# A fused hybrid layer on one core: projection in segments of two, two and four blocks, the first one in the query weights' room

## The chip, the core and the metric

The kernel runs on one core of a Trainium2 chip as one launch. The metric is the device time of that core in microseconds. Before the change the median of three runs is 3722.16 us (3713.23 to 3744.35).

## The reference: what is computed

One layer over 1024 tokens of width 1024, float32, cut here to its stages:

```python
h = rms_norm(x, norm1_w)
proj = h @ w_in                     # 1024 -> 3592 columns
sq, sk = rms_norm(q), rms_norm(k)   # 8 attention heads of 64
o_sb  = rms_norm(stick_breaking_attention(sq, sk, sv))
qkv   = silu(causal_depthwise_conv(gdn_qkv))          # 4 taps
gq, gk = l2_normalize(gq) * 128**-0.5, l2_normalize(gk)
o_gdn = rms_norm(gated_delta_net(gq, gk, gv, decay, write)) * silu(gate)
x = x + concat(o_sb, o_gdn) @ w_out
hn = rms_norm(x)
q = hn @ peer_w_q                   # 8 heads x 2 halves x 128
# top 16 of 128 keys per half, top 16 of the 256 sums -> 128 experts per token
act = gelu(u_table[experts] . hn) * softmax(best)
y = x + sum(act * v_table[experts])
```

Attention is causal over blocks of 128 tokens, the delta net carries a state from block to block, and the convolution needs the last three tokens of the columns before. Every token reads 128 rows of 4 KB from the table u and 128 from v.

## The kernel before, in words

**Tiles.** The 1024 tokens are 8 blocks of 128. Two blocks form a segment (`SEG = 2`, line 38), so there are four segments. `projection(g)` computes all input projections of a segment and writes them to scratch tensors in device memory (`d_gqT`, `d_gkT`, `d_gv`, `d_qT`, `d_kT`, `d_v`, `d_gate`, `d_ab`). `mixing(b)` then runs one block: delta net ("start", "level", "state" in the list of points), attention over b+1 key blocks ("key"), output projection ("mix", "out"), the second norm ("hn"), the query projection with the resident 8 MB of `w_q` and the key scores ("pq", "score"), and the top-16 selections ("top"). The order is segment 0, blocks 0 and 1, segment 1, blocks 2 and 3, segment 2, and so on.

**A projection step.** The 3584 columns are 28 chunks of 128 (`CH`, line 46), of the kinds g (query and key of the delta net), v, s (attention query and key), a (attention value) and z (gate). One step is one chunk for the two blocks: 8 matmuls with a result of 128 x 256, an evacuation on ACT, for g and v a convolution of four taps on DVE, for g, v and z a silu on ACT and DVE, for g and s a norm. These stages trail the matmul by one to six steps, and nine more steps drain them. Weights come in pairs of chunks of 1 MB. Segment 0 reads them from `w_in` in runs of 1 KB through four slots and also saves them to `d_w`; later segments read them back from `d_w` through two slots. SP issues all of these loads and stores in one order: the load of pair j+2 is issued when pair j is through the matmuls, behind the stores of the steps before.

**Room.** `work` (24 tiles of 512 columns) holds a segment's tiles during a projection and a block's tiles during mixing, so the loads of block 0's delta net wait for the whole projection (line 537). `w_q_t` is filled after segment 0 and scaled once by the second norm's weights on ACT (line 951).

**Gathers.** POOL issues 1024 gathers from u and 1024 from v, one column of indices each: 128 rows of 4 KB, 512 KB. DVE takes each u row block's dot product with the normed tokens (line 1072) and frees its slot of `u_ring` (9 slots). PE sums the v rows with weights that ACT spreads into `column`, and frees its slot of `v_ring` (8 slots). The gathers of block b are spread by a table over the work on later blocks: `points()` gives every place in the program a weight, `MARKS` (line 144) gives pairs of (block, share of its stretch, u rows done, v rows done), and `table()` interpolates. At each point DVE, ACT, PE and POOL process rows up to the table's number. After block 7 only rows are left ("last"). Every engine runs its instructions strictly in this written order.

**Ahead of a segment.** In the "top" part of the block before, the segment's token blocks are loaded, squared, scaled and turned (`x_loads`, `x_squares`, `x_scale`, `x_turns`, `x_copies`); PE waits in `x_turns` for the scaled blocks.

Of the kernel before, what the change touches and what calls it, by code (L numbers as in the profile page):

```python
# [36 lines left out]

SEG = 2
ST = SEG * P
NSEG = NB // SEG  # L40
# [3 lines left out]
NP = len(PAIRS)  # L44

# [7 lines left out]
def number(kinds, n):  # L53
    return sum(CH[m][0] in kinds for m in range(n + 1))


def conv_count(n):
    return number("gv", n)


def silu_count(n):
    return number("gvz", n)


def norm_count(n):
    return number("gs", n)


Z0 = min(n for n in range(NCH) if CH[n][0] == "z")


def needs_tokens(n):
    return CH[n][0] == "v"


def stored(n):
    return CH[n][0] != "v"


def token_count(n):  # L80
    return sum(needs_tokens(m) for m in range(n + 1))


def stores_before(n, slot):
    return sum(stored(m) for m in range(slot, n, 4))


NORMS, CONVS, SILUS, TOKS = norm_count(NCH - 1), conv_count(NCH - 1), silu_count(NCH - 1), token_count(NCH - 1)
# [30 lines left out]
def segment_before(b):  # L119

    return b // SEG if b >= 2 and b % SEG == 0 else None


def token_turn_pending(n):

    return any(0 <= m < NCH and needs_tokens(m) for m in (n - 7, n - 8))


def points():


    for b in range(1, NB):
        if segment_before(b) is not None:
            for n in range(NCH + 9):
                yield ("p", segment_before(b), n), 5.0 if n < NCH else 2.5, None if n < 4 or token_turn_pending(n) else 1
# [8 lines left out]
MARKS = [(1, 0.62, 128, 0), (1, 1.0, 128, 40), (2, 1.0, 250, 118), (4, 1.0, 500, 368), (6, 1.0, 756, 624), (7, 1.0, 884, 750)]  # L144
# [57 lines left out]
def hybrid_layer_kernel(nc, x, norm1_w, w_in, sb_q_norm_w, sb_k_norm_w, sb_out_norm_w, gdn_conv_w,  # L202
# [9 lines left out]
    d_w = scratch("d_w", (NP, P, KC * 256))  # L212
# [12 lines left out]
    with ctx:  # L225
# [53 lines left out]

        xT = work[:, 0:KC * ST].rearrange("p (k t) -> p k t", k=KC)  # L280
        w_work = [work[:, 2048 * n:2048 * (n + 1)].rearrange("p (k c) -> p k c", k=KC) for n in (2, 1)]
        v_flat = v_ring[:, :, :].rearrange("p s d -> p (s d)")
        w_v = [v_flat[:, 2048 * n:2048 * (n + 1)].rearrange("p (k c) -> p k c", k=KC) for n in range(PW_FIRST - PW)]
        w_slots = [w_work[0], *w_v, w_work[1]]
        A0 = 6144

        def tile_a(n):
            return work[:, A0 + n * ST:A0 + (n + 1) * ST]


        x_seg = work[:, 2048:2048 + SEG * D].rearrange("p (n d) -> p n d", n=SEG)
        x_scratch = work[:, 0:D]
        s_ring = [tile_a(n) for n in range(6)] + [tile_a(20)]
        e_ring = [tile_a(6 + n) for n in range(2)]
        sq_ring = [tile_a(8 + n) for n in range(2)]
        y_ring = [tile_a(10 + n) for n in range(2)]
        o_ring = [tile_a(12 + n) for n in range(4)]
        tok_ring = [tile_a(16 + n) for n in range(2)]
        tmp_a = [tile_a(18), tile_a(19)]
        cb = [work[:, A0 + 21 * ST + n * 264:A0 + 21 * ST + n * 264 + ST + 3] for n in range(2)]  # L300
# [4 lines left out]
        ab_bank = bank(ox, 1)[:, 0:16]  # L305
        AB = A0 + 21 * ST + 2 * 264
        ab_out, ab_e = work[:, AB:AB + 16], work[:, AB + 16:AB + 32]
        ab_y = work[:, AB + 32:AB + 40]
        ab3 = ab_bank.rearrange("p (b c) -> p b c", b=SEG)
        ab_y3, ab_e3 = ab_y.rearrange("p (b c) -> p b c", b=SEG), ab_e[:, 8:16].rearrange("p (b c) -> p b c", b=SEG)  # L310
        ab_o3 = ab_out.rearrange("p (b c) -> p b c", b=SEG)

        u_flat = u_ring[:, :, :].rearrange("p s d -> p (s d)")
# [158 lines left out]
        def w_slot(g, j):  # L472
            return w_slots[slot_of(g, j)[0]]
# [1334 lines left out]
```

## Time and profile before

| | |
|---|---|
| median of three runs | 3722.16 us |
| the profiled execution | 3719.36 us, of which the span is 3717.5 us |
| granted TensorE clock, mean | 0.774 |
| busy, of the span | PE 66%, DVE 63%, POOL 62%, ACT 23% |
| bytes moved | 1267.87 MB, 341 GB/s over the span |
| the gathers' queue | 1073.87 MB, 77.1% of 16 DMA engines' time |

The DMA share is the mean busy share of the core's 16 DMA engines; it can pass 1 where several queues' packets overlap. A stage's row gives busy microseconds and, in brackets, the number of instructions of each engine in that stretch. POOL's number counts the gathers it issued. The stretches start and end at marks in the trace: segments at the block before's last selection, blocks at the first operation of their delta net.

### The profile page before, as it was taken

What the parts mean: (1) busy time and instruction counts of PE and PEld (TensorE: products, weight loads), DVE (VectorE), ACT (ScalarE), POOL (GpSimd) and SP (SyncE); (2) the same over time, 40 slices, a digit from 0 to 9 for tenths busy, and PEclk for the clock granted to TensorE, in tenths of its full rate; (3) what the DMA queues carried; (4) which work ended last, traced back from release to release, by engine and by line L of the source; (5) the groups of instructions that cost most, each with busy time, mean ns of one, the idle gap of its engine ahead of it and who ended that gap; (6) DMA issues with size and microseconds to landing.
All of it is one profiled execution on the core that took longest, in us unless ns stands there. A gap on an engine that the chain in (4) does not pass through costs nothing.

```text
span 3717.5 us, 46890 instructions
## 1 busy us (share of the span) xinstructions
PE 2447.1 (66%) x16321; PEld 1511.2 (41%) x16321; DVE 2333.5 (63%) x5581; ACT 862.8 (23%) x2400; POOL 2323.0 (62%) x2091
## 2 busy tenths in 40 slices
PE   7672546967747858668657868568757863544466
PEld 6562433644524536344434546344434440100123
DVE  4439875777676577666777677656876567444300
ACT  4330112332113123223114223223113211110112
POOL 0004774565556667766666766766777777777765
PEclk9786577988867979788778979788767785555588
DMA  7725998998889999999989999999999999999999
GB/s 242 252 77 191 338 327 312 348 361 310 306 281 367 357 345 413 406 387 384 359 319 392 345 369 414 404 365 363 348 331 391 370 330 356 377 364 376 355 375 336
DMA packets 392250, 1267.87 MB, mean 341 GB/s; under 512 B 43789, under 2 KB 95058, under 8 KB 382802
## 3 DMA queue, kind: packets, MB, share of 16 engines
q0 software_dynamic: 294912, 1073.87, 77.1%
q1 hardware_dynamic: 78674, 149.06, 11.1%
q10 hardware_dynamic: 18432, 41.95, 3.1%
q8 instruction: 132, 2.16, 0.2%
q14 instruction: 100, 0.82, 0.1%
HBM read 1225.89 MB, written 38.83 MB: 340 GB/s over the span
## 4 chain that ended last, share of the span: by engine, by line
PE 33%; DVE 24%; issue 12%; POOL 12%; DMA 6%; another core or an unknown queue 6%; ACT 3%; DVEq 3%; ACTq 1%; SPq 0%; POOLq 0%
PE zz L1520 16%; PE va L1520 10%; DVE u_ring L1072 8%; POOL u_ring L683 7%; POOL v_ring L698 5%; PE rr L1520 4%; DMA v_ring<-in_peer_v,idxT 3%; PE ox L1520 2%; DMA u_ring<-in_peer_u,idx 2%; DMA work<-d_w 1%; DVE work L1405 1%; DVE work L1407 1%; DVE work L1129 1%; DVE work L1288 1%
## 5 line engine op out<-in xcount | busy, mean ns | idle before, releaser
L683 POOL DMA_INDIRECT u_ring<-in_peer_u,idx x1024 | 1187.1, 1159 | 856.0 <-issue 293.0
L1072 DVE SCALAR_TENSOR_TENSOR u_ring<-u_ring,hn_t 128x1024 f32<-128x1024 f32 x1024 | 1216.9, 1222 | 316.4 <-DMA u_ring<-in_peer_u,idx 270.0
L698 POOL DMA_INDIRECT v_ring<-in_peer_v,idxT x960 | 1066.8, 1111 | 497.2 <-issue 234.1
L1520 PE MATMUL va<-v_ring,column 128*32 128x256 f32 x7680 | 809.3, 479 | 518.2 <-DMA v_ring<-in_peer_v,idxT 329.8
L1520 PE MATMUL zz<-work 128*128 128x256 f32 (+3 forms) x3232 | 738.5, 390 | 128.4 <-issue 50.5
L1520 PEld LDWEIGHTS zz<-work 128*128 128x128 f32 (+1 forms) x3232 | 551.9, 212 | 339.6 <-issue 202.7
L1520 PEld LDWEIGHTS va<-v_ring,column 128*32 128x32 f32 x7680 | 247.8, 124 | 1009.7 <-DMA v_ring<-in_peer_v,idxT 484.6
L762 ACT ACTIVATE column<-onehot,wT 128x32 f32<-128x32 f32 x1024 | 279.4, 314 | 917.0 <-PE va L1520 513.3
L1520 PE MATMUL rr<-work,w_q_t 128*128 128x128 f32 x1024 | 140.7, 291 | 18.5 <-issue 17.4
L1520 PE MATMUL rr<-work,later 128*128 128x512 f32 x144 | 102.3, 818 | 76.6 <-issue 35.2
L1520 PEld LDWEIGHTS rr<-work,w_q_t 128*128 128x128 f32 x1024 | 130.8, 204 | 31.2 <-issue 29.9
L1520 PE MATMUL zz<-work,w_q_t 128*128 128x128 f32 x1024 | 127.9, 283 | 8.0 <-issue 7.7
L1476 DVE TENSOR_TENSOR y_buf<-va,y_buf 128x1024 f32<-128x1024 f32 x8 | 9.8, 1221 | 194.4 <-PE va L1520 194.0
L1520 PEld LDWEIGHTS zz<-work,w_q_t 128*128 128x128 f32 x1024 | 122.1, 198 | 18.5 <-issue 18.5
L1520 PE MATMUL rr<-work 128*128 128x128 f32 x640 | 102.5, 314 | 22.2 <-DVE work L1244 6.7
L1520 PE MATMUL ox<-work 128*128 128x64 f32 (+1 forms) x704 | 99.8, 298 | 20.1 <-ACT work L931 18.9
L1520 PEld LDWEIGHTS ox<-work 128*128 128x128 f32 x704 | 92.8, 211 | 42.2 <-issue 42.0
L1520 PEld LDWEIGHTS rr<-work 128*128 128x128 f32 x640 | 93.2, 225 | 36.2 <-issue 15.7
L1524 PE MATMUL zz<-ident,work 128*128 128x128 f32 x40 | 11.3, 428 | 146.2 <-DVE work L1414 83.6
L1270 DVE SCALAR_TENSOR_TENSOR work<-zz,work 128x512 f32<-128x512 f32 x72 | 49.4, 686 | 77.8 <-ACT work L923 43.9
L1277 DVE SCALAR_TENSOR_TENSOR work<-zz,work 128x512 f32<-128x512 f32 x72 | 49.3, 685 | 55.4 <-remote 37.4
L1072 DVE DVE_READ_ACCUMULATOR u_ring<-u_ring,hn_t 128x1 f32 x1024 | 83.1, 81 | 0.0
(247 smaller groups left out, 2513.2 us busy)
## 6 DMA issues: line engine op xcount, KB each, us to landing
work<-d_w SPq DMA_DIRECT2D x42, 1024.0 KB
work<-in_w_out ACTq DMA_DIRECT2D x64, 512.0 KB
u_ring<-in_peer_u,idx POOLq DMA_INDIRECT x1024
v_ring<-in_peer_v,idxT POOLq DMA_INDIRECT x960
work<-d_kT SPq DMA_DIRECT2D x36, 256.0 KB
work<-d_v SPq DMA_DIRECT2D x36, 256.0 KB
work<-in_x SPq DMA_DIRECT2D x16, 512.0 KB
w_q_t<-in_peer_w_q SPq DMA_DIRECT2D x1, 8192.0 KB, 27.3
```

The costliest lines, as they stand in the source:

```text
L683: g.indirect_dma_start(u_ring[:, n % RU, :], None, u_rows, bass.IndirectOffsetOnAxis(idx[b % 2][:, s:s + 1], 0)).then_inc(u_landed[n % RU] ...
L698: g.indirect_dma_start(v_row(n), None, v_rows, bass.IndirectOffsetOnAxis(idxT[b % 3][:, t:t + 1], 0)).then_inc(v_landed[slot] if slot < RV ...
L762: a.activation(column[:, m % RC, :], onehot[:, 31 - g:63 - g], ACT.Copy, scale=wT[b % 2][:, 32 * k + g:32 * k + g + 1]).then_inc(column_do ...
L1072: v.scalar_tensor_tensor(u_ring[:, m % RU, :], u_ring[:, m % RU, :], 1.0, hn_t[b % 2][:, :], ALU.mult, ALU.mult, accum_out=dots[:, s:s + 1 ...
L1129: last = v.scalar_tensor_tensor(s_ring[n % 7], cb[c % 2][:, k:k + ST], vecs[:, w[k]:w[k] + 1], s_ring[n % 7], ALU.mult, ALU.add)
L1270: sp = v.scalar_tensor_tensor(att_sp[hg], bank(zz, hg), 0.0, att_l[hg], ALU.max, ALU.add)
L1277: v.scalar_tensor_tensor(att_u[hg], bank(zz, hg), 0.0, att_l[hg], ALU.min, ALU.subtract).then_inc(z_used, 1)
L1288: arg = v.tensor_tensor(att_u[hg], att_u[hg], bank(rr, hg), ALU.subtract)
L1405: v.tensor_tensor(hot[half], hot[half], top_f[:, of, c, :].unsqueeze(2).to_broadcast(shape), ALU.mult)
L1407: v.tensor_reduce(e[:, of], hot[half], AX.X, ALU.add)
L1520: return t_.matmul(out_, lhsT, rhs, start=start, stop=stop, skip_group_check=True)
L1524: last = t_.transpose(dst[:, c * P:(c + 1) * P], src[:, c * P:(c + 1) * P], ident[:, :])
```

## The change

The segments are 2, 2 and 4 blocks (`SIZES`). A step stays one chunk of 128 columns for two blocks; the segment of four runs every chunk twice, once for each pair of blocks ("halves"), so it has 56 steps plus 9. Its weights come from `d_w` as single chunks of 512 KB, each used by two steps. `d_w` is now stored by chunk. For the kinds a and z a step was 256 columns of one block; now it is 128 columns of both, in 16 matmuls of 128 columns instead of 8 of 256. The tiles of a segment are an `Area`: segment 0's lies in `w_q_t`, the others' in `work`. Block 0's delta-net loads are issued once the g and v chunks are stored; `w_q` is loaded after the projection, and is no longer scaled: instead the turned hidden state is scaled when it is copied, in four operations on ACT and four on DVE in every block. The turns of the two sub-key tables move from after segment 0 into block 0's mixing. The four token blocks of the last segment are prepared in block 3's selections. `MARKS` has new entries.

```diff
-SEG = 2
-ST = SEG * P
-NSEG = NB // SEG
+SIZES = (2, 2, 4)
+B0 = [sum(SIZES[:g]) for g in range(len(SIZES) + 1)]
+NSEG = len(SIZES)
+ST = 2 * P
...
-MARKS = [(1, 0.62, 128, 0), (1, 1.0, 128, 40), (2, 1.0, 250, 118), (4, 1.0, 500, 368), (6, 1.0, 756, 624), (7, 1.0, 884, 750)]
+MARKS = [(1, 0.62, 128, 0), (1, 1.0, 128, 40), (2, 1.0, 250, 118), (3, 1.0, 339, 207), (4, 1.0, 500, 374), (6, 1.0, 744, 596),
+         (7, 1.0, 884, 750)]
...
-    d_w = scratch("d_w", (NP, P, KC * 256))
+    d_w = scratch("d_w", (NCH, P, KC * P))
...
+                if size == 2:
+                    self.xT = [columns(base[:, 0:2048], ST)]
+                    self.w_slots = [base[:, 4096:6144], v_flat[:, 0:2048], v_flat[:, 2048:4096], base[:, 2048:4096]]
+                else:
+                    self.xT = [columns(base[:, 0:2048], ST), columns(base[:, 4096:6144], ST)]
+                    self.w_slots = [base[:, 2048:3072], None, None, base[:, 3072:4096]]
...
+        areas = [Area(w_q_t if g == 0 else work, SIZES[g]) for g in range(NSEG)]
...
                 if j >= ahead:
-                    sp.wait_ge(projected, NCH * g + 2 * (j - ahead) + 2)
-                elif j == ahead - 1:
-                    sp.wait_ge(x_turned, SEG * (g + 1))
+                    sp.wait_ge(projected, G.steps0 + 2 * (j - ahead) + 2)
+                elif j == ahead - 1 or G.halves == 2:
+                    sp.wait_ge(x_turned, B0[g + 1])
...
+                    for c in range(2):
+                        sp.dma_start(columns(w_slot(g, j)[:, 1024 * c:1024 * c + 1024], P),
+                                     w_in[0].rearrange("(k p) n -> p k n", p=P)[:, :, col + P * c:col + P * c + P]).then_inc(
+                                         w_landed[slot], 8 * 2)
+                elif G.unit == 2:
+                    sp.dma_start(columns(w_slot(g, j), KC * P),
+                                 d_w[2 * j:2 * j + 2].rearrange("h p c -> p h c")).then_inc(w_landed[slot], 16)
                 else:
-                    src = d_w[j].rearrange("p (k c) -> p k c", k=KC)
-                sp.dma_start(w_slot(g, j), src).then_inc(w_landed[slot], 16)
+                    sp.dma_start(w_slot(g, j), d_w[j]).then_inc(w_landed[slot], 16)
...
-                    if n == Z0 + 4:
-                        sp.wait_ge(projected, NCH * (g + 1))
...
+                    if g == 0 and n == G.gv_end + 5:
...
+                        gdn_loads(0)
+                    if g and n == G.steps:
...
             def x_scale(g):
                 act.wait_ge(x_meaned, 2 * g + 2)
-                for n in range(SEG):
-                    a.activation(x_seg[:, n, :], x_seg[:, n, :], ACT.Copy, scale=r8[:, n:n + 1]).then_inc(x_scaled, 1)
+                for n in areas[g].x_order:
+                    x = areas[g].x_rows[n]
+                    a.activation(x, x, ACT.Copy, scale=r8[:, n:n + 1]).then_inc(x_scaled, 1)
...
-                if b == 0:
-                    act.wait_ge(wq_landed, 16)
-                    for k in range(KC):
-                        a.activation(w_q_sb[:, k, :], w_q_sb[:, k, :], ACT.Copy, scale=vecs[:, R_N2 + k:R_N2 + k + 1])
...
-                a.activation(hT[:, 0:512], bank(rr, 0), ACT.Copy).then_inc(hT_act, 1)
+                for k in range(4):
+                    last = a.activation(hT[:, k * P:(k + 1) * P], bank(rr, 0)[:, k * P:(k + 1) * P], ACT.Copy,
+                                        scale=vecs[:, R_N2 + k:R_N2 + k + 1])
+                last.then_inc(hT_act, 1)
...
-                        for k in range(KC):
-                            if kind in "az":
-                                last = mm(mm_bank[n % 2], xT[:, k, P * (n % 2):P * (n % 2) + P], wc[:, k, :], k == 0, k == KC - 1)
-                            else:
-                                last = mm(mm_bank[n % 2], wc[:, k, P * (n % 2):P * (n % 2) + P], xT[:, k, :], k == 0, k == KC - 1)
+                        if kind in "az":
+                            for p in range(2):
+                                for k in range(KC):
+                                    last = mm(mm_bank[n % 2][:, P * p:P * p + P], x[:, k, P * p:P * p + P], wc[:, k, :],
+                                              k == 0, k == KC - 1)
+                        else:
+                            for k in range(KC):
+                                last = mm(mm_bank[n % 2], wc[:, k, :], x[:, k, :], k == 0, k == KC - 1)
...
+                if b == 0:
+                    pe.wait_ge(sub_landed, 32)
+                    turn(va[:, :], sub_in[0], PH).then_inc(sub_turned, 1)
...
-                    if q == 2 and g is not None:
-                        pe.wait_ge(xT_act, SEG * (g + 1))
+                    if q == 2 and g is not None and SIZES[g] == 4:
+                        x_turns(g, 1)
+                    if q == 3 and g is not None:
+                        pe.wait_ge(xT_act, B0[g + 1])
```

The table of rows, done (u, v) at the end of each stage, as the two programs compute it: up to block 3 both have (339, 207). Before: segment 2 (406, 274), block 4 (500, 368), block 5 (593, 461), segment 3 (658, 526), block 6 (756, 624), block 7 (884, 750). Changed: the segment of four (431, 302), block 4 (500, 374), block 5 (619, 482), block 6 (744, 596), block 7 (884, 743). Both end at (1024, 1024).

**How the instructions move.** SP at the end of segment 0, before the change (`w_q_t` is the query weights' room, `d_subT` the turned sub-keys):

```order
L504 DMA d_w<-v_ring 128x2048 [waits w_landed1]
L527 DMA d_kT<-work 128x2x128 [waits normed]
L531 DMA d_v<-work 128x256 [waits normed] x2
L569 DMA ab_in<-d_ab 128x8 [waits o_stored3,tok_stored0,o_stored2,tok_stored1,o_stored1,ab_stored,o_stored0,projected]
L569 DMA work<-d_gkT 128x512
L569 DMA work<-d_gqT 128x512
L569 DMA work<-d_gv 128x512
L531 DMA d_gate<-work 128x256 [waits normed] x4
```

and after it:

```order
L643 DMA ab_in<-d_ab 128x8 [waits tok_stored0,o_stored3,tok_stored1,o_stored2,ab_stored,o_stored1,o_stored0]
L643 DMA work<-d_gkT 128x512
L643 DMA work<-d_gqT 128x512
L643 DMA work<-d_gv 128x512
L569 DMA d_w<-v_ring 128x2x1024 [waits w_landed1]
L599 DMA d_kT<-w_q_t 128x2x128 [waits normed]
L599 DMA d_v<-w_q_t 128x2x128 [waits normed] x2
L599 DMA d_gate<-w_q_t 128x2x128 [waits normed] x4
```

The four loads of block 0 now stand before the last weight save and the last stores of values and gates, and no longer wait for the last matmul.

PE in block 3's selections, where the tokens of the third segment are turned, before:

```order
L1524 MATMUL zz<-ident,work 128x128 [waits x_scaled,sc_copied]
L1524 MATMUL zz<-ident,work 128x128 x7
L1524 MATMUL rr<-ident,work 128x128 [waits x_scaled]
L1524 MATMUL rr<-ident,work 128x128 x7
L1520 MATMUL va<-v_ring,column 32x256 [waits column_done,v_landed6]
```

and after the change:

```order
968 L1617 MATMUL rr<-ident,work 128x128 [waits x_scaled]
969 L1617 MATMUL rr<-ident,work 128x128 x7
970 L1613 MATMUL va<-v_ring,column 32x256 [waits column_done,v_landed6]
971 L1613 MATMUL va<-v_ring,column 32x256 x3
972 L1613 MATMUL va<-v_ring,column 32x256 [waits column_done,v_landed7]
973 L1613 MATMUL va<-v_ring,column 32x256 x3
974 L1613 MATMUL va<-v_ring,column 32x256 [waits column_done,v_landed0]
975 L1613 MATMUL va<-v_ring,column 32x256 x3
976 L1617 MATMUL zz<-ident,work 128x128 [waits x_scaled,xT_act]
977 L1617 MATMUL zz<-ident,work 128x128 x7
978 L1617 MATMUL rr<-ident,work 128x128 [waits x_scaled]
979 L1617 MATMUL rr<-ident,work 128x128 x7
```

A second pair of turns follows three v rows later and waits for ACT's copies of the first pair.

## Rows read from the trace of the kernel before

**Rows 1.** Busy time by stage: stretch, length, engines, clock, DMA share, GB/s.

```profile
16.00:142.00 126.00, 111.76 (x520) 95.87 (x520) 61.91 (x171) 49.35 (x140) 0.00 (x0) 0.99 0.70 230
...
622.00:820.00 198.00, 144.21 (x825) 103.65 (x825) 129.14 (x295) 60.58 (x183) 111.02 (x100) 0.89 0.92 344
820.00:1057.00 237.00, 151.51 (x1037) 102.29 (x1037) 177.14 (x466) 45.19 (x117) 133.11 (x115) 0.78 0.84 303
1057.00:1352.00 295.00, 199.21 (x1454) 125.07 (x1454) 204.81 (x517) 68.48 (x190) 190.64 (x171) 0.80 0.93 343
1352.00:1568.00 216.00, 170.68 (x1049) 116.59 (x1049) 153.44 (x337) 69.28 (x221) 157.91 (x138) 0.87 1.03 407
1568.00:1877.00 309.00, 202.58 (x1525) 124.07 (x1525) 214.28 (x527) 66.85 (x180) 214.00 (x190) 0.80 0.97 370
1877.00:2180.00 303.00, 215.72 (x1566) 135.16 (x1566) 217.63 (x538) 79.29 (x210) 206.46 (x182) 0.83 0.95 356
2180.00:2392.00 212.00, 166.78 (x1042) 114.71 (x1042) 151.57 (x336) 68.92 (x219) 150.58 (x133) 0.89 1.03 407
2392.00:2720.00 328.00, 232.62 (x1630) 138.90 (x1630) 227.27 (x549) 78.36 (x201) 227.81 (x199) 0.78 0.97 361
2720.00:3117.00 397.00, 272.64 (x1894) 156.95 (x1894) 264.63 (x610) 88.94 (x233) 287.00 (x250) 0.76 0.96 357
3117.00:3517.00 400.00, 178.75 (x1130) 39.80 (x1129) 183.47 (x305) 43.53 (x146) 300.07 (x279) 0.52 0.98 367
```

**Rows 2.** Timeline of DVE at the end of segment 0 (start us, us, what).

```profile
152.53 0.07 DVE L1483 MEMSET sm<- 128x8 f32 x1
...
158.10 0.16 DVE L1188 COPY sm<-ab_in 64x4 f32<-64x4 f32 x1 [5.50 <-DMA work<-d_gv]
```

**Rows 3.** Timeline of SP there.

```profile
152.55 0.32 SPq L569 DMA_DIRECT2D ab_in<-d_ab  x1
```

**Rows 4.** Timeline of ACT in block 0, from the output projection on.

```profile
233.05 1.14 ACT L943 ACTIVATE work<-rr,vecs 128x128 f32<-128x128 f32 x4 [3.51 <-PE rr L1524]
...
234.07 15.24 ACT L951 ACTIVATE w_q_t<-w_q_t,vecs 128x2048 f32<-128x2048 f32 x8
...
253.14 0.60 ACT L957 ACTIVATE work<-rr 128x512 f32<-128x512 f32 x1
```

**Rows 5.** Timeline of PE there.

```profile
234.25 16.37 PE L1520 MATMUL zz<-work 128*128 128x512 f32 x32 [1.23 <-ACT work L943]
...
253.16 2.05 PE L1520 MATMUL ox<-work,ones 128*128 128x128 f32 x16
```

**Rows 6.** Two windows of 10 us while PE waits to turn tokens (block 3).

```profile
1320.00:1330.00 10.00, 0.00 (x0) 0.00 (x0) 9.46 (x53) 1.04 (x5) 7.29 (x7) 0.50 0.96 347
1330.00:1340.00 10.00, 3.37 (x16) 3.28 (x16) 9.03 (x43) 4.21 (x11) 0.00 (x0) 0.50 0.27 109
```

**Rows 7.** Timeline of PE there: one v row's matmuls, then the turn.

```profile
1302.44 0.64 PE L1520 MATMUL va<-v_ring,column 128*32 128x256 f32 x8 [0.90 <-DMA v_ring<-in_peer_v,idxT]
...
1336.63 1.94 PE L1524 MATMUL zz<-ident,work 128*128 128x128 f32 x8 [26.31 <-ACT work L786]
```

**Rows 8.** Timeline of ACT: first and last evacuation of segments 1 and 2.

```profile
649.78 0.38 ACT L816 ACTIVATE work<-zz 128x256 f32<-128x256 f32 x1 [6.25 <-PE zz L1520]
...
794.26 0.38 ACT L811 ACTIVATE work<-zz 128x256 f32<-128x256 f32 x1 [1.76 <-DVE work L1166]
...
1357.59 0.38 ACT L816 ACTIVATE work<-zz 128x256 f32<-128x256 f32 x1 [4.82 <-issue]
...
1538.18 0.39 ACT L811 ACTIVATE work<-zz 128x256 f32<-128x256 f32 x1 [1.56 <-PE zz L1520]
```

**Rows 9.** The chain in segment 2: a weight load.

```profile
1452.24 9.91 DMA work<-d_w
```

**Rows 10.** Windows: rows of 1 KB alone, then of 8 KB alone.

```profile
12.00:16.00 4.00, 1.96 (x10) 1.62 (x8) 0.00 (x0) 3.58 (x15) 0.00 (x0) 1.00 1.10 359
...
170.00:185.00 15.00, 8.65 (x36) 7.69 (x36) 7.15 (x11) 1.79 (x3) 0.00 (x0) 0.54 1.01 423
```

More of the change, by code:

```diff
@@ L88, with __init__, at, kind @@
-NORMS, CONVS, SILUS, TOKS = norm_count(NCH - 1), conv_count(NCH - 1), silu_count(NCH - 1), token_count(NCH - 1)
+class Segment:
+    def __init__(self, g, before):
+        self.b0, self.size, self.halves = B0[g], SIZES[g], SIZES[g] // 2
+        self.steps = NCH * self.halves
+        self.unit = 2 // self.halves
+        self.units = NCH // self.unit
+        self.steps0 = before.steps0 + before.steps if before else 0
+        self.convs0 = before.convs0 + before.convs(before.steps - 1) if before else 0
+        self.silus0 = before.silus0 + before.silus(before.steps - 1) if before else 0
+        self.norms0 = before.norms0 + before.norms(before.steps - 1) if before else 0
+        self.toks0 = before.toks0 + before.toks if before else 0
+        self.stores0 = [before.stored_in(q) if before else 0 for q in range(4)]
+        self.toks = self.tokens(self.steps - 1)
+        self.gv_end = max(n for n in range(self.steps) if self.kind(n) in "gv") + 1
+        self.norm_end = max(n for n in range(self.steps) if self.kind(n) in "gs") + 1
+        self.z_first = min(n for n in range(self.steps) if self.kind(n) == "z")
+    def at(self, n):
+        return CH[n // self.halves]
+    def kind(self, n):
+        return CH[n // self.halves][0]
+    def half(self, n):
+        return n % self.halves
+    def number(self, kinds, n):
+        return sum(self.kind(m) in kinds for m in range(n + 1))
+    def convs(self, n):
+        return self.number("gv", n)
+    def silus(self, n):
+        return self.number("gvz", n)
+    def norms(self, n):
+        return self.number("gs", n)
+    def is_v(self, n):
+        return self.kind(n) == "v"
+    def tokens(self, n):
+        return self.number("v", n)
+    def stores(self, n, slot):
+        return sum(not self.is_v(m) for m in range(slot, n, 4))
+    def stored_in(self, slot):
+        return self.stores0[slot] + self.stores(self.steps, slot)
+    def turn_pending(self, n):
+        return any(0 <= m < self.steps and self.is_v(m) for m in (n - 7, n - 8))
@@ L91, in v_slot @@
+SEGS = []
+for _g in range(NSEG):
+    SEGS.append(Segment(_g, SEGS[-1] if SEGS else None))
+HIST = {n: i for i, n in enumerate(n for n in range(NCH) if CH[n][0] in "gv")}
 def v_slot(m):
@@ L119, in segment_before @@
 def segment_before(b):
[L121 to L126 removed]
+    return B0.index(b) if b and b in B0 else None
 def points():
@@ L291, in hybrid_layer_kernel, with columns @@
[L291 to L300, printed above, removed]
+        def columns(ap, n):
+            return ap.rearrange("p (k c) -> p k c", c=n)
@@ L996, in mixing @@
                 at("top", 3)
+                if g is not None and SIZES[g] == 4:
+                    x_copies(g, 1)
                 act.wait_ge(best_shifted, b + 1)
```

439 lines of the change are left out of this document (236 added, 203 removed).

## The prediction

> **What bounds the kernel now.** Read the stages first [rows 1]. Segment 0 runs on PE: 111.76 us busy of 126, at a clock of 0.99, and no gather can start before block 0 has chosen experts. From segment 2 on the DMA share is 0.95 to 1.03 and PE, DVE and POOL all have room, so the late kernel is paced by the transfers. The gathers' price is read from the last stage, where nothing else runs: 414 rows from 3117 to the span's end at 3717.5 is 1.45 us a row. The reader is to see two further things. The transfer rate is no constant: 407 GB/s in segments 2 and 3, 356 to 370 in the blocks, 367 with rows alone. And segment 1, with only 87 rows to gather by the table, ran at 344 GB/s and still took 198 us; that is what a segment costs when its own work is the limit. Then the places where engines wait: the end of segment 0 on DVE and SP [rows 2, 3], PE waiting to turn the next segment's tokens [rows 6, 7], the rate of steps [rows 8] and a weight load's landing [rows 9].
>
> One profiled execution gives the durations. Its time is 3719.4 us, 2.8 below the median of the three runs; its span is 3717.5.
>
> **The start.** DVE is through with segment 0 at 152.53 and waits 5.50 us, to 158.10, for block 0's loads, which SP issued at 152.55 [rows 2, 3]. Now they stand before the last stores and need only the g and v chunks, which are stored several steps earlier; the room they land in is free because segment 0 lives elsewhere. DVE's own end stays, so 5.5 us go, and everything behind, the first gather included, moves with it. Next to be late there is DVE. What is added at the start I cost at nothing, with its cover:
> - `w_in` in runs of 512 bytes. DMA is busy 0.70 of 126 us, so 38 us are free [rows 1]. Runs of 1 KB moved at 359 GB/s, runs of 8 KB at 423 [rows 10]: an eightfold cut cost 15% of the rate. 14.7 MB at 359 are 41 us; another halving costs 0 to, were each packet's time not to fall at all, 41 us. I take a few, under cover; the upper end would add some 3 us.
> - the scaling of `w_q` (15.24 us of ACT) lay beside the output projection (16.37 us of PE), so its removal gives 0 [rows 4, 5]. Four scaled copies cost 1.14 us where one plain copy cost 0.60 [rows 4]; they lie beside PE's 2.05 us of norm weights [rows 5]. 0, at most 0.5 us in each of eight blocks, +4.
> - the sub-key turns lie in PE's idle time of block 0; x for block 0 is now loaded behind their stores, some 12 us before it is added. 0; +3 if the stores land late.
> - a and z steps: 16 matmuls of 128 columns for 8 of 256, the same columns. 8 of 128 took 2.05 us [rows 5], so 16 take at most 4.1 us where a step has 4.0 of PE (111.76 / 28) [rows 1]. 0 to +0.5 us on 32 steps; 0, since most run under the transfers.
> - `d_w` in runs of 4 KB for 8, in both segments that read it: 14.7 MB at 367 instead of 423 GB/s is 5 us of transfers in segment 1, which has share 0.92: 0 to +5 [rows 1, 10].
>
> Up to the end of block 3 the table of rows is the same within one row.
>
> **Preparing four blocks.** Before segment 2 PE stood 26.31 us until ACT had scaled the tokens; v's ring filled, and POOL issued no gather in ten microseconds, with the rate at 109 GB/s [rows 6, 7]. Segment 3's preparation in block 5 did about the same. The first stays; ACT now scales four blocks before it copies, a second pair of turns waits for the copies of the first, and the first weights wait for all four turns. Between 0 and 15 us; I take +5, the price of ACT's two extra scalings and of 16 extra copies on it. The second stall, some 9 us, goes with its segment and is in the rates below.
>
> **The segment of four.** It has 56 steps and 187 rows, where segment 2 had 28 steps and 134. Transfers: 187 x 0.524 = 98 MB, weights 14.7, stores 7.3, together 120 MB; at 410 GB/s that is 293 us, the lower end. Its own work: segment 1's first and last evacuations lie 144.5 us apart, 5.35 us a step [rows 8]. There PE needed 4.0 us and one v row of 0.64 [rows 1, 7]; now it needs 4.0 + 1.6 x 0.64 = 5.0. Against that, a load of 1 MB took 9.91 us on the chain where two steps of lead are 10.7, and the loads are now half as large [rows 9]. So a step is between 5.0 and 5.7 us; I take 5.3. 55 x 5.3 = 292, and 35 us of start and drain as in segment 2 (1352 to 1357.6, 1538.2 to 1568): **327 us**. It is 34 us above what the transfers need, and in that the change gives back what it saves: one reading of the weights, 14.7 MB, is 36 us at 407 GB/s.
>
> The Trainium skill (DMA: Bandwidth & Descriptors, Measured) says to batch transfers to at least 1 MiB and gives 6.15 us for 1 MB; its anatomy section fits 2.0 us plus the bytes at 436 GB/s, by which 28 loads of 512 KB need 28 us more than 14 of twice the size need beyond the same bytes. By that the sum would be 28 us higher; by the row, which shows 407 GB/s in a stage made almost only of 512 KB gathers, nothing.
>
> **Block 4.** 141 rows instead of 188. If every row gave its full 1.45 us, 309 - 68 = 241, the lower end; if a third of that, 286. Block 2, with 113 rows and share 0.84, took 237: on the line between the two blocks (0.96 us a row) it is 264. I take 258, near that line, a little down because two thirds of what goes is still paced by transfers.
>
> **Blocks 5 to 7.** 227, 239 and 287 rows instead of 186, 196 and 254. Their other transfers are what the stage rows leave: 303 x 0.356 - 182 x 0.524 = 12.4 MB, and likewise 14.1 and 10.6 [rows 1]. Together 432 MB. The rates were 356, 361 and 357; more rows for the same work push them towards the 367 of rows alone, and block 5 loses its preparation stall. At 367: **1177 us**; at 358, 1206; at 370, 1167.
>
> **The last rows.** 421 x 1.45 = 611 us, for 600.5.
>
> Sum from 1352: 327 + 258 + 1177 + 611 = 2373, where it was 216 + 309 + 303 + 212 + 328 + 397 + 600.5 = 2365.5, so +7.5. With -5.5 and +5: 3719.4 + 7 = **3726 us**.
>
> **The rivals.**
>
> *The transfers stay the limit throughout* (22%). The segment of four takes its 293 us, block 4 241, blocks 5 to 7 1167: 2312, 53.5 less; with the start 3719.4 - 53.5 - 5.5 = 3660. For it: DMA share 0.92 in segment 1 already, and half-size loads end the landing on the chain. Against it: 344 GB/s there, and 303 in block 2.
>
> *A step stays as long as in segment 2* (17%). Its evacuations are 180.6 us apart, 6.69 us a step [rows 8], read above as the price of four rows a step. If it is instead the handing of a step through PE, ACT, DVE and back next to v rows, four steps of one kind in a row making it worse, 55 x 6.69 + 35 = 403 us, 76 more: 3802. It decides from 5.9 us a step on, where the sum passes 3759. Against it: segment 1's 5.35 with the same chain.
>
> *Half a load takes as long as a whole one* (5%): with 9.91 us to land and a microsecond or two behind stores on SP's queue, a pair of steps can't be under 11.6 us, 1 us over 10.6, 28 times: 3754. [...]
>
> *The early loads bring nothing* (6%), because DVE's last copies, which wait for stores, move back behind them on the queue: 3731.
>
> The forecast itself has 50%.
>
> **The numbers.** What a measurement of this kernel tells from no change is 1%, 37 us. Faster by more, under 3685: the first rival, 0.22. Slower by more, over 3759: the second, and half of the third with the forecast's bad end, 0.21. Within: 0.57. The range reaches half of the way to each of the outer cases and holds the unknown costs: the segment at 5.0 to 5.7 us a step is -17 to +22, block 4 -17 to +28, the rates -10 to +29, the start 0 to +15. They will not all fall to one side; 3675 to 3775.
>
> **What would show it.** DVE's first copy of block 0 near 152.7, with no wait for the loads. The first and last of 56 evacuations about 290 us apart, at 360 to 375 GB/s, below the 407 of before, and block 4 below 350. POOL's gathers per microsecond higher in blocks 5 to 7 than before. The prediction is wrong if the segment of four runs at 400 GB/s (then it is faster) or if its steps take over 5.9 us. A single stall at the second pair of turns of over 15 us would also break it.

## The result, and the profile after

The changed kernel takes 3778.28 us (median of 4 runs, 3771.42 to 3786.29), the kernel before 3726.72 us beside it: a ratio of 1.0133, 95% interval 1.0098 to 1.0168. A second time, beside 23 runs of the kernel before, it was 1.0152 (1.0115 to 1.0189). So it is slower by 50 us or so, and the forecast of 3726 us and its range up to 3775 missed it.

The stages of the changed kernel, with the columns of [rows 1]; its profiled execution has a span of 3769.7 us:

```profile
16.00:142.00 126.00, 112.58 (x648) 100.64 (x648) 61.56 (x170) 49.27 (x140) 0.00 (x0) 0.99 0.77 236
...
610.00:812.00 202.00, 153.99 (x962) 112.20 (x961) 129.48 (x296) 60.54 (x183) 111.15 (x101) 0.86 0.92 340
812.00:1054.00 242.00, 155.24 (x1037) 104.62 (x1037) 177.37 (x466) 45.74 (x120) 131.57 (x113) 0.76 0.82 297
1054.00:1342.00 288.00, 200.53 (x1470) 130.08 (x1470) 205.86 (x523) 77.91 (x215) 193.76 (x172) 0.80 0.94 348
1342.00:1709.00 367.00, 306.40 (x2058) 229.05 (x2057) 249.32 (x569) 127.30 (x392) 216.77 (x194) 0.91 0.93 340
1709.00:1967.00 258.00, 182.02 (x1341) 117.04 (x1341) 185.28 (x481) 61.89 (x163) 154.47 (x142) 0.80 0.91 337
1967.00:2330.00 363.00, 237.11 (x1671) 140.38 (x1671) 251.93 (x596) 77.26 (x209) 254.77 (x228) 0.77 0.96 359
2330.00:2705.00 375.00, 252.25 (x1758) 149.65 (x1758) 261.81 (x611) 83.16 (x222) 272.35 (x237) 0.77 0.98 366
2705.00:3154.00 449.00, 294.37 (x2061) 165.51 (x2061) 279.01 (x640) 95.49 (x256) 314.23 (x283) 0.76 0.95 353
3154.00:3554.00 400.00, 166.92 (x1138) 42.56 (x1138) 174.38 (x288) 43.83 (x149) 292.60 (x277) 0.53 0.97 367
```

The reader is to see where the two kernels part. Up to the third segment the changed one is 10 us ahead (1342 for 1352). The segment of four (1342 to 1709) takes 367 us at 340 GB/s, where the two segments that it replaces ran at 407 [rows 1]. The account is short with the table of rows. Before, segment 2, blocks 4 and 5 and segment 3 took 216 + 309 + 303 + 212 = 1040 us and did 638 rows. Now the segment of four with blocks 4 and 5 takes 367 + 258 + 363 = 988 us and does 555. The 52 us saved leave 83 rows for later, and from there to the end it is 375 + 449 + 615.7 = 1439.7 us, where it was 328 + 397 + 600.5 = 1325.5: 114 us, 1.38 a row. -10 - 52 + 114 is the 52 us between the spans. A second pair of traces (e12 and e14 below) has 982 us for 1059 in the first sum and 1439 for 1325 in the second, and its third segment begins at 1345 for 1347. So the 114 us come back, the 52 are 52 to 78, and the 10 us ahead are scatter: over nine traces that point lies at 1345 to 1352 with the kernel before and the version of experiment 5, and at 1342 to 1353 with the segment of four.

The transfers moved in forty equal slices of the steps in segment 2 of the kernel before (1358 to 1538):

```profile
GB/s 295 424 414 410 409 409 424 405 407 412 410 410 418 407 422 410 423 408 411 401 416 411 422 407 420 410 426 410 412 411 411 407 427 405 415 417 403 405 408 412
```

and in the segment of four (1352 to 1690):

```profile
GB/s 411 191 335 323 369 396 411 335 284 275 402 285 265 267 293 377 411 415 394 343 348 379 315 123 346 348 397 256 307 283 270 295 299 401 412 412 340 370 404 354
```

Before, every slice but the first stands at 401 to 427. In the segment of four nine of forty pass 400; the others stand between 123 and 397. The waits there, in total, times and longest, say who holds the transfers back:

```profile
POOL v_ring L773 <- PE va L1613: 57.7, 27, 8.6
POOL u_ring L758 <- DVE u_ring L1156: 42.3, 16, 4.5
```

The same two waits in segment 2 of the kernel before:

```profile
POOL u_ring L683 <- DVE u_ring L1072: 11.4, 5, 4.2
...
POOL v_ring L698 <- PE va L1520: 4.5, 6, 2.3
```

POOL, which issues the gathers, stood 100 us of 338 for a slot that PE or DVE had not yet freed; before it was 16 of 180. The rows are asked for too late because the engines that eat them are late. The chain by line gives PE's projection first, with 36.7% in the segment of four and 29.6% in segment 2 before, where a weight load (`work<-d_w`) had 5.5%; it is gone from the head of the chain after the change.

PE itself, from the first to the last evacuation, is idle 40.4 us by the list of its waits. The two largest stand before the turns of the v chunks, which need DVE's copy of the finished chunk and, from ACT, the evacuation of the turn before:

```profile
PE ox L1617 <- DVE work L1257: 12.3, 2, 6.8
PE ox L1617 <- ACT work L939: 11.0, 6, 2.3
```

The sums of the norms wait another 9.1 us for DVE. The v rows and the turn of their weights wait 6.3 us; 1.7 us before projection matmuls have no releaser in the trace. No wait of PE or DVE between 1352 and 1690 names a gather or a weight load (35 us in six waits of ACT's evacuations have an unknown releaser), so by the waits the transfers don't hold this stage.

The DMA share of 0.93 seems to speak against that, but it falls less than the rate: divided by the share, the rate is 366 GB/s here (340 / 0.93), 395 in segment 2 before (407 / 1.03), and 319 in the segment of experiment 2 that has hardly a gather (118 / 0.37). So a high share is here no sign that no more could be moved. Why the quotient falls is not shown; the shorter runs are at most a small part of it, since e1 and e13 have them too and move 387 to 405 GB/s in their third and fourth segments.

The first and last of the 56 evacuations, as in [rows 8]:

```profile
1352.47 0.38 ACT L894 ACTIVATE work<-zz 128x256 f32<-128x256 f32 x1 [6.58 <-issue]
...
1686.49 0.38 ACT L889 ACTIVATE work<-zz 128x256 f32<-128x256 f32 x1 [0.54 <-issue]
```

334.0 us for 55 steps, **6.07 us a step** where 5.3 was forecast. The second trace of the same kernel (e12) has 1352.61 and 1693.28, 6.19.

### The profile page after: what moved, and what is told of

It reads as the page before. It is cut to its first block, busy times and chain, and to the rows that moved or that the text cites. A ratio compares the mean times of both kernels' runs of the same rounds, so it can differ in the third digit from the quotient of the medians.

```text
span 3769.7 us, 47941 instructions
## 1 busy us (share of the span) xinstructions
PE 2469.2 (66%) x16833; PEld 1552.5 (41%) x16833; DVE 2333.3 (62%) x5592; ACT 853.1 (23%) x2411; POOL 2293.2 (61%) x2091
## 2 busy tenths in 40 slices
DMA packets 414496, 1253.28 MB, mean 332 GB/s; under 512 B 44013, under 2 KB 113714, under 8 KB 412210
## 3 DMA queue, kind: packets, MB, share of 16 engines
q1 hardware_dynamic: 100914, 134.38, 10.4%
## 4 chain that ended last, share of the span: by engine, by line
PE 31%; DVE 26%; issue 13%; POOL 12%; DMA 6%; another core or an unknown queue 5%; ACT 4%; DVEq 3%; ACTq 1%; SPq 0%; POOLq 0%
PE zz L1613 14%; DVE u_ring L1156 9%; PE va L1613 9%; POOL u_ring L758 6%; POOL v_ring L773 5%; PE rr L1613 4%; DMA v_ring<-in_peer_v,idxT 4%; PE ox L1613 2%; DMA u_ring<-in_peer_u,idx 1%; DVE work L1218 1%; DVE work L1377 1%; DVE work L1497 1%; DVE work L1499 1%; DVE work L1359 1%
## 5 line engine op out<-in xcount | busy, mean ns | idle before, releaser
L773 POOL DMA_INDIRECT v_ring<-in_peer_v,idxT x960 | 1048.5, 1092 | 552.1 <-issue 237.6
L1613 PE MATMUL zz<-work 128*128 128x128 f32 (+3 forms) x3392 | 686.9, 364 | 121.0 <-issue 50.5
L1613 PEld LDWEIGHTS zz<-work 128*128 128x128 f32 (+1 forms) x3392 | 524.4, 210 | 318.0 <-issue 211.7
L1359 DVE SCALAR_TENSOR_TENSOR work<-zz,work 128x512 f32<-128x512 f32 x72 | 49.5, 687 | 95.7 <-ACT work L1005 56.7
L1613 PE MATMUL va<-u_ring,column 128*32 128x256 f32 x512 | 71.1, 498 | 21.3 <-issue 19.2
```

What stands on the lines that cost most here:

```text
L773: g.indirect_dma_start(v_row(n), None, v_rows, bass.IndirectOffsetOnAxis(idxT[b % 3][:, t:t + 1], 0)).then_inc(v_landed[slot] if slot < RV ...
L1359: sp = v.scalar_tensor_tensor(att_sp[hg], bank(zz, hg), 0.0, att_l[hg], ALU.max, ALU.add)
L1613: return t_.matmul(out_, lhsT, rhs, start=start, stop=stop, skip_group_check=True)
```

## The experiments

Jobs differ in their level: the kernel before took 3722 to 3728 us in all but one, and 3500 in that one (below). A ratio is always to the kernel before in the same job. Stage times are of one profiled execution each. T is the theory that the segment of four is bound by its own work with the rows in it; the expectations name its rivals.

**1. Segments of 2, 2, 2 and 2 with every other edit kept** (e1, and again as e13).

```diff
-SIZES = (2, 2, 4)
+SIZES = (2, 2, 2, 2)
-MARKS = [(1, 0.62, 128, 0), (1, 1.0, 128, 40), (2, 1.0, 250, 118), (3, 1.0, 339, 207), (4, 1.0, 500, 374), (6, 1.0, 744, 596),
-         (7, 1.0, 884, 750)]
+MARKS = [(1, 0.62, 128, 0), (1, 1.0, 128, 40), (2, 1.0, 250, 118), (4, 1.0, 500, 368), (6, 1.0, 756, 624), (7, 1.0, 884, 750)]
```

> The changed kernel with segments of 2, 2, 2 and 2 blocks and the table of rows (MARKS) of before: everything of the change but the segment of four. Theory A (the loss is made in the segment of four, whose 56 steps took 6.07 us each where I had 5.3, and in what follows from it): the early start gives 4 to 6 us, the rest costs nothing, 3722 minus 5, so 3712 to 3722. Rival (the small edits cost: d_w in runs of 4 KB, 16 matmuls of 128 columns for a and z, four scaled copies a block): segment 1 was 4 us longer and block 2 5 us longer in the changed kernel, which over four segments and eight blocks makes 20 to 40 us: 3735 to 3755.

Measured: 1.0049 (1.0017 to 1.0081), 3741.7 us, as its rival had it, and the second time

> e1_sizes2222 a second time, to stand beside e10_start_alone (0.9979) and e11_stores (1.0003) if the kernel before takes about 3500 us here, and beside its own 1.0049 if it takes 3722. Theory: the small edits cost what they did, ratio 1.002 to 1.007, and the stores' runs of 512 bytes are a part of it. Rival: on a faster memory they cost nothing, ratio 1.000 to 1.001, as e11_stores.

1.0003 (0.9974 to 1.0031), outside the 1.002 to 1.007 of its theory, though the kernel before took 3728 us there and not 3500. The two together put all the small edits, the gain of the early start counted in, at between nothing and 0.5%; which, they don't settle. Against the changed kernel's 1.0133 and 1.0152 the size of the last segment, with its table, holds the larger part: 1.0133 to 1.0049 is 0.8%, 31 us, and 1.0152 to 1.0003, in one job, 1.5%, 56 us. The table of rows goes back with the size, so the two are not parted here.

**2. The rows taken out of the segment of four** (e4; 15 rows in it instead of 187, the others behind it).

```diff
-MARKS = [..., (3, 1.0, 339, 207), (4, 1.0, 500, 374), ...]
+MARKS = [..., (3, 1.0, 339, 207), (4, 0.572, 346, 215), (4, 1.0, 500, 374), ...]
```

> The changed kernel with a table of rows that gives the segment of four only 15 rows (0.3 a step instead of 3.1) and block 4 all the others. Its step is then the segment's own price. Theory C and rival R both expect 4.5 to 5.0 us a step, as segment 0 has (4.5), and the time gets longer by 60 to 120 us, since the transfers idle. Third theory S (the segment's own handing is slow: loads of half the size, two halves to a chunk): over 5.3 us a step without rows.

3926.0 us in one run, a span of 3924.3. Its own steps, and the changed kernel's between its first and last evacuation:

```profile
1358.00:1624.00 266.00, 236.87 (x1336) 206.47 (x1335) 137.45 (x368) 102.98 (x287) 17.86 (x18) 0.94 0.37 118
```

```profile
1352.00:1686.00 334.00, 293.31 (x1975) 221.30 (x1977) 229.74 (x528) 120.34 (x369) 191.97 (x172) 0.93 0.93 336
```

Almost without rows and with the transfers at 118 GB/s a step still takes 266.3 / 55 = 4.84 us, within the 4.5 to 5.0 expected; theory S (over 5.3) is out. So 4.84 of the 6.07 us are there with the transfers mostly idle. PE is busy 236.87 / 55 = 4.31 of them and idle 0.53, all of it in waits for DVE and ACT. With rows it is busy 293.31 / 55 = 5.33; the 639 matmuls more are 80 v rows (8 records each), and PE's idle time grows to 0.74. So 6.07 = 4.31 as without rows + 1.02 that came with them + 0.74 of handing over. By matmul, the v rows take 54.2 us there, 86.5 of them at 0.63, which is 0.99 a step; e4 itself holds 7 (0.09 a step).

The rows taken out made the segment 79 us shorter (288 us for 367), 0.46 a row, and everything behind it 226 us longer, 1.31 a row: block 4 took 428 us, 170 more, block 5 411, 48 more. The time grew by 148 us, over the 60 to 120 expected.

**3. More rows in the segment of four** (e6; 228 instead of 187, 31 fewer in block 4).

```diff
-MARKS = [..., (3, 1.0, 339, 207), (4, 1.0, 500, 374), ...]
+MARKS = [..., (3, 1.0, 339, 207), (4, 0.572, 452, 322), (4, 1.0, 504, 380), ...]
```

> The changed kernel with another table of rows: 228 instead of 187 rows in the segment of four (3.9 instead of 3.1 a step), 110 instead of 141 in block 4, the rest nearly as it was. Theory M (the segment is too thinly filled: without rows its step takes 4.84 us, with 3.1 rows 6.07, so a row costs 0.4 us there, while in a block it costs about 1 us): segment 367 to about 385 us at 385 GB/s, block 4 258 to about 230, blocks 5 on 15 us less for ten rows fewer; the time falls from 3778 to 3745 to 3760. Rival K (what the segment gains, block 4 loses, since both live on the 173 u rows of blocks up to 3 that are known by then; block 4 has its own floor near 250 us): 3765 to 3785.

1.0145 (1.008 to 1.0211), 3781 us, as rival K had it. The segment took 402 us, a step 6.77, block 4 234.5. In this trace, of the slowest of its four executions (3801.59 us), a row cost 0.85 us in the segment and saved 0.76 in block 4. No gain shows from moving rows between these two stages. Tables that fill block 5 instead, or leave fewer rows for the end, were not tried.

**4. The order of kinds in the segment of four** (e2: the kinds alternate chunk by chunk, two steps each, instead of four of one kind in a row; e7: this and the marks of e6).

```diff
+ORDER4 = [2 * p + j for j in range(2) for p in range(NP - 2)] + list(range(NCH - 4, NCH))
...
-        return CH[n // self.halves]
+        return CH[self.chunk(n)]
+
+    def chunk(self, n):
+        return ORDER4[n // 2] if self.halves == 2 else n
...
-                    sp.dma_start(w_slot(g, j), d_w[j]).then_inc(w_landed[slot], 16)
+                    sp.dma_start(w_slot(g, j), d_w[ORDER4[j]]).then_inc(w_landed[slot], 16)
...
```

> The changed kernel with the 28 chunks of the segment of four in another order: the kinds alternate chunk by chunk (g s v g s a ...), so that no more than two steps of one kind follow each other, as in the segments of two. Theory C (four g or v steps in a row overload DVE: convolution, silu, norm and row come to 6.5 to 7 us each, PE then waits for the result): steps fall from 6.07 to about 5.4 us, the segment from 367 to 330 us, the time from 3778 to 3740 to 3755. Rival R (a step's length comes from its three rows handed in between, in whatever order the kinds stand): steps stay at 5.9 to 6.2 us, the time within 10 us of 3778.

> Both together: the alternating order of chunks in the segment of four (which took its stretch from 367 to 347 us) and the fuller table of rows. Theory M: 3730 to 3748, still no faster than before, since the transfers' spare time in segment and block 4 is only moved. Rival K: like the order alone, 3760 to 3775.

e2 1.0101 (1.0029 to 1.0172), 3769 us; e7 1.011 (1.0077 to 1.0144), 3762 us, as rival K had it. In e2 the steps went down to 5.84 us, between theory C (5.4) and rival R (5.9 to 6.2), and the segment to 350 us at 353 GB/s. In e7 a step took 6.45 us where e6 has 6.77. So the order is worth some 0.2 to 0.35 us a step. From the segment on to the end e2 took 2415 us, the two traces of the changed kernel 2428 and 2421: of the 17 to 19 us of the segment 5 to 13 are left, and block 6 alone took 390 us for 375 and 381. Both ratios lie inside the changed kernel's first interval, and their intervals overlap the second, so a gain in the total isn't shown.

**5. The same question in the kernel before** (e5: its kinds in fours).

```diff
-PAIRS = [("g", 0), ("s", 0), ("v", 0), ("g", 1), ("s", 1), ("a", 0), ("g", 2), ("s", 2), ("v", 1), ("g", 3), ("s", 3),
+PAIRS = [("g", 0), ("g", 1), ("s", 0), ("s", 1), ("v", 0), ("v", 1), ("g", 2), ("g", 3), ("s", 2), ("s", 3), ("a", 0),
```

> The kernel before with its pairs of chunks in an order that puts four steps of one kind in a row (g g s s v v g g s s a a z z by pairs), the cadence of the segment of four, and nothing else. Theory C: the g and v stretches of segments 1 to 3 get longer than PE and the transfers can hide; 8 to 20 us more for each of the three, 4 to 8 for segment 0: 3745 to 3790. Rival R: the order doesn't matter, 3715 to 3730.

1.0003 (0.9976 to 1.003), as rival R had it, segment 2 at 219 us and 400 GB/s. Four steps of a kind in a row cost nothing in the total there, where the transfers run at 400. With e2 this leaves the order a small part of the 6.07 us, and not the main cause of the loss.

**6. The small edits by themselves**, each in e1's kernel: `d_w` back in runs of 8 KB (e8); the a and z steps back to 8 matmuls of 256 columns with stores of 1 KB (e9); both (e10); only those stores (e11).

```diff
 # e8, e10
-    d_w = scratch("d_w", (NCH, P, KC * P))
+    d_w = scratch("d_w", (NP, P, 2 * KC * P))
...
 # e9, e10, e11
-                            at = (d_v if kind == "a" else d_gate)[bm:bm + 2, :, P * c:P * c + P].rearrange("b t c -> t b c")
+                            at = (d_v if kind == "a" else d_gate)[b0 + c % 2][:, 256 * (c // 2):256 * (c // 2) + 256]
...
 # e9, e10
-                            for p in range(2):
-                                for k in range(KC):
-                                    last = mm(mm_bank[n % 2][:, P * p:P * p + P], x[:, k, P * p:P * p + P], wc[:, k, :],
-                                              k == 0, k == KC - 1)
+                            both = w_slot(g, unit).rearrange("p (c k n) -> p k c n", c=2, k=KC)
+                            for k in range(KC):
+                                last = mm(mm_bank[n % 2].rearrange("p (c n) -> p c n", c=2),
+                                          x[:, k, P * (n % 2):P * (n % 2) + P], both[:, k, :, :], k == 0, k == KC - 1)
```

> The kernel with segments of 2, 2, 2, 2 (which ran 0.5% over the kernel before, with its segments 4, 12 and 7 us longer) with one edit taken back: d_w again in runs of 8 KB for a pair of chunks. Theory P (twice the packets for 14.7 MB in each of three segments whose transfers are the limit): segments back to 198, 216, 212 us within 4, the time 15 to 20 us under that kernel's 3742, so 3720 to 3728. Rival Q (it is the a and z steps or the scaled copies): 3735 to 3748, segments as long as there.

> The same kernel of 2, 2, 2, 2 with the other edit taken back instead: a and z steps again 8 matmuls of 256 columns for one block, and their stores again in runs of 1 KB. Theory P: no change from 3742 (3735 to 3748). Rival Q: 3720 to 3728, with the a and z steps of the segments shorter.

> The changed kernel with segments of 2, 2, 2 and 2 blocks and the table of rows of before, its a and z steps as before (8 matmuls of 256 columns of one block, stores in runs of 1 KB), and d_w in runs of 8 KB as before. What stays of the change is segment 0 in the room of w_q with block 0's loads early, w_in in runs of 512 bytes, and the scaling of the turned hidden state instead of w_q. Reading of the runs so far: small edits add up, each price by itself: e9 gave 3715.6, 0.6% under e1_sizes2222, and e8 3728.8, 0.3% under it. If the two prices add, this one is at 3705 to 3715, 0.2 to 0.5% faster than before (the early start, worth 4 to 6 us, is then a real gain). Rival: they do not add, since both only free transfers in the same saturated stages, or e9's gain is scatter between programs; then it is at 3716 to 3725, no different from before, and the early start is given back. Segments 1, 2 and 3 should take 190 to 200, 215 to 222, 209 to 220 us.

> e1_sizes2222 with the stores of the a and z steps alone taken back to runs of 1 KB; the steps keep their 16 matmuls of 128 columns of both blocks (so the stored values and gates stand in wrong columns, and the attention's output and the experts chosen are other ones, of the same number). It parts the two halves of what e9 took back. If the runs of 512 bytes in stores, and the same bytes' loads, are the price, this is at 3715 to 3720 as e9 is. If the form of the matmuls is (twice as many weight loads of PE beside the v rows in the same step), it stays at 3735 to 3742 as e1_sizes2222 is. PE busy in segment 2 should stay within 1 us of e1_sizes2222's in both cases.

e8 1.0028 (1.0003 to 1.0053), 3728.8 us, just over its theory P; e9 0.9989 (0.9959 to 1.0019), 3715.6 us, below both of its ranges. e10 0.9979 (0.9969 to 0.9989) and e11 1.0003 (0.9991 to 1.0014) in one job, whose level makes their expected times void. e10 is the early start with what it needs: segment 0 in `w_q`'s room, `w_in` in runs of 512 bytes, the scaling of the turned hidden state. It is the one version whose whole interval lies under the kernel before, by 0.2% (3496.82 us for 3500.54). Against e11, which stores values and gates in wrong columns and of which only the time counts, it takes back the matmuls' form and the runs of 8 KB, and is 0.24% lower; e11's stores alone can't be priced, since e1 has no ratio at this level. e9 was the only one to speak for the a and z steps, beside an e1 whose own 1.0049 did not come back.

In this job the kernel before took 3500.54 us. With rows alone, e10 and the changed kernel's second trace (another job):

```profile
3000.00:3400.00 400.00, 192.10 (x1465) 39.05 (x1465) 155.80 (x254) 57.61 (x186) 303.38 (x312) 0.51 1.03 406
```

```profile
3143.00:3543.00 400.00, 171.70 (x1138) 43.92 (x1138) 173.25 (x285) 43.70 (x148) 291.98 (x280) 0.55 0.98 368
```

406 GB/s for 368, with 312 gathers issued in 400 us for 280: on another chip, rows alone move 10% faster. Why is not shown.

**7. Both kernels again, each with a trace** (e12 the changed one, e14 the one before).

> The changed kernel, unchanged, a second time beside the kernel before. Where the kernel before takes about 3722 us, the ratio should be 1.0133 again, 1.010 to 1.017. In the last two runs the kernel before took 3500.5 us and rows alone moved at 409 GB/s instead of 367 (measured in the last stage of e10_start_alone). Theory T (a step of the segment of four is bound by its own work plus what each row adds, the transfers stand partly idle there): at such a rate the segment keeps its 360 to 370 us while what it leaves undone is worth less, 1.28 us a row instead of 1.45, and block 4 with few rows stays near 250; the idle capacity is 409 minus 340 of 409 in 367 us, 62 us, where it was 60, so the loss stays 45 to 60 us, a ratio of 1.013 to 1.018. Rival: the loss is in the transfers' own efficiency (shorter runs, queues), then it shrinks with them, to 0 to 30 us, a ratio under 1.009.

> The kernel before, unchanged, with a trace of its own on this chip: ratio 1.000, within 0.003. If it takes about 3500 us, its stages are those of e10_start_alone within 3 us each (segment 2 at 217 us, block 4 at 283, last rows at 409 GB/s), so the whole difference of 222 us lies in stages that the transfers pace, and segment 0 and block 0 do not differ. If the difference were in the engines, segment 0 would be shorter too.

e12 1.0152 (1.0115 to 1.0189), e14 1.0002 (0.9966 to 1.0037). The loss is there again, and both ratios lie within what was expected. e12's segment of four:

```profile
1345.00:1713.00 368.00, 306.85 (x2062) 228.39 (x2058) 249.39 (x568) 127.50 (x392) 217.33 (x192) 0.91 0.93 336
```

368 us as before. Its block 4 took 249 us for 258, so a single stage can differ by 9 us between two executions. e14's segment 2 took 219 us at 403 GB/s. The changed kernel did not run on the chip with the faster rows, so T's claim for it and its rival's stay open.

## Why the prediction was wrong

**The segment of four** is the step that failed: "a step is between 5.0 and 5.7 us; I take 5.3". It was 6.07 and the stage 367 us for 327, which is 40 of the 45 us by which the profiled span (3769.7) passed the forecast sum (3724.5 as a span). The term for v rows was right: 1.6 rows at 0.64 were forecast, 1.57 at 0.63 measured. Two others were not. A step's own work on PE was taken at 4.0 us from segment 0 and is 4.31 in e4. Of these 0.3 us, 0.09 are e4's few v rows, 0.1 are longer projection matmuls (395 ns a record of 256 columns on average, for 380 to 392 in segment 0, at a granted clock of 0.94 for 0.99; with the rows it is 405 ns at 0.93), and most of the rest are the matmuls for `d_ab`. And 0.3 us were left for PE's idle time, which is 0.74. Idle time of 0.5 was there to be read: segment 1 was PE 129 us busy of 144,

```profile
650.00:794.00 144.00, 129.18 (x736) 96.00 (x728) 111.01 (x257) 54.38 (x164) 78.10 (x69) 0.99 0.94 352
```

so each of its 5.35 us held 4.78 of work (129.18 / 27) and 0.57 of handing over. Added to the forecast's own 5.0 this makes 5.57, and with the measured 4.31 for 4.0 it is 5.88, at the threshold of 5.9 that the second rival had. So the kind of limit was forecast, PE's work plus handing over, and the size of two of its terms was not.

**The second rival**, "a step stays as long as in segment 2", had 17%, and its mechanism is the one that acted: the handing of a step through the engines next to the rows. Its size, 6.69 us, was too high, and its "four steps of one kind in a row" is worth 0.2 to 0.35 us (experiment 4). It came out on the right side. The measured steps grow with the rows that the table gives a step, drain included, but not in one line: 4.84 us at 0.2 (e4), 5.35 at 2.4 (segment 1 before), 6.07 and 6.19 at 2.9, 6.77 at 3.5 (e6), 6.69 at 3.6 (segment 2 before). Segment 2's 6.69, then, could be read in both ways, as the price of transfers and as that of its rows; I took only the first. e6 has nearly the same length at 354 GB/s.

**The start**: forecast 5.5 us. From the last evacuation of segment 0 to the first operation of block 0 it was 143.47 to 158.10, 14.6 us, and is 10.4 (143.89 to 154.26):

```profile
153.10 1.06 DVE L1257 COPY w_q_t<-w_q_t 128x256 f32<-128x256 f32 x3 [1.75 <-DMA d_kT<-w_q_t]
...
154.26 0.16 DVE L1277 COPY sm<-ab_in 64x4 f32<-64x4 f32 x1
```

DVE waits for no load, as forecast, and 1.75 us for a store that now stands behind the loads, the fourth rival's mechanism in small. Over twelve traces with the early loads this stretch is 9.9 to 10.9 us, over three without 13.7 to 14.6: 4 us are gained. Segment 0's own end moves by 7 us from one execution to the next (142.8 to 150.1), in both forms, and hides that in a single trace.

**Edits costed at nothing.** Segment 0 had PE busy 112.58 us for 111.76, with a DMA share of 0.77 for 0.70: runs of 512 bytes stayed covered. The removed scaling of `w_q` gave little or nothing: block 0 took 166.1 us for 167.8, and 166.4 in e5, which still has it. Segment 1 took 202 us for 198 (+5 was the bound for 4 KB runs), block 2 242 for 237; in e12 191 and 241. Over six traces with the segment of four, segment 1 takes 190 to 204 us, over the three of the old form 197 to 201: no price shows in it. Together 0 to 0.5% (experiment 1).

**Preparing four blocks**: forecast +5. PE turned the first pair of blocks at 1326.56 after 20.09 us, the second at 1334.32 after 2.19:

```profile
1326.56 1.94 PE L1617 MATMUL zz<-ident,work 128*128 128x128 f32 x8 [20.09 <-ACT work L862]
1334.32 1.74 PE L1617 MATMUL zz<-ident,work 128*128 128x128 f32 x8 [2.19 <-ACT work L871]
```

Block 3's stage took 288 us for 295, and 292 for 286 in e12 and e14. No loss shows, and the +5 is not shown either.

**Block 4, blocks 5 to 7, the last rows**: 258, 1187 and 616 us against 258, 1177 and 611. These 15 us over and the 40 of the segment make 55, and the 10 us by which the segment began earlier bring it to 45. That block 4 was met to the microsecond is luck in part: e12 has 249. **Half a load as long as a whole one** (5%): between 1352 and 1690, where 26 of the 28 loads were issued, no engine's wait names `d_w`, and the longest gap without a releaser before PE takes up projection weights is 0.8 us. The rule of the Trainium skill on batches of 1 MiB (DMA: Bandwidth & Descriptors, Measured) set no limit here: those loads of 512 KB cost PE no wait. So the 28 us that the prediction reckoned from the same page do not show in the segment's 40.

The first rival, transfers as the limit throughout, had 22% and needed 400 GB/s. The saving of 14.7 MB was real (1253.28 MB for 1267.87), but in a stage at 340 GB/s, where no wait of PE or DVE names a transfer, it bought nothing that shows.

## What to carry to other kernels

Where a transfer-bound program has stretches with much engine work, making such a stretch do more work with fewer bytes can move it off the transfer limit, as here; count the rows that stay undone there, at the price that it has later (here 83 rows at 1.38 us against 52 us saved). For a step's length read busy and idle time of its tightest engine in the closest stage, and keep the idle time as a term: it grew from 0.53 to 0.74 us a step with the rows beside it. And keep one thing apart from another when packing edits: the early start with what it needs gave 0.2%, and the segment that came with it cost more than that.

## What was not expected of the hardware

The same kernel before took 3500 us in one job and 3722 to 3728 in the others. Rows of 4 KB alone moved at 406 GB/s there and 367 here, while the segments stood near 407 in both: segment 2 took 216 us in e10 as in the kernel before. And in the job at 3500 us the kernel before scattered far less (3496.62 to 3509.99 over 23 runs) than in the last one (3702.99 to 3750.31 over 23), so 0.2% could be told there and not here.

The DMA share passes 1 with a single queue too: in the 4 us of [rows 10] with runs of 1 KB one queue alone comes to 109.7% of the sixteen engines' time, at 359 GB/s.
